# Two trunk layers on one core: the cached context's keys and values of the second mixer expanded between the last expert and the first projection

## The reference, cut to what matters

```python
def mla_expand(ckv, kpe, w_ukv, g_k):
    kv = (ckv @ w_ukv).reshape(bn, n, C_HEADS, C_NOPE + C_V)
    k_nope, v = kv[..., :C_NOPE], kv[..., C_NOPE:]
    k = jnp.concatenate([k_nope, jnp.broadcast_to(kpe[:, :, None, :], ...)], -1)
    return rms_norm(k, g_k), v

# odd_mixer
z = h @ p['w_in']                                # 1024 -> 384 + 256 + 32
q = rms_norm((rms_norm(cq, p['g_qa']) @ p['w_uq']).reshape(bn, n, C_HEADS, C_QK), p['g_q'])
k, v = mla_expand(rms_norm(ckv, p['g_kva']), kpe, p['w_ukv'], p['g_k'])
...                                              # rotary positions for latent tokens
kc, vc = mla_expand(ctx[0], ctx[1], p['w_ukv'], p['g_k'])
out = dense_attention(q, concat([kc, k]), concat([vc, v]), C_SCALE, None)
```

## Time and profile before

| what | value |
|---|---|
| median of 3 runs | 1086.15 us (1083.31 to 1087.44) |
| the profiled execution | 1081.3 us |
| its span in the profile | 1079.5 us |
| PE busy | 913.2 us, 85% |
| DVE busy | 387.9 us, 36% |
| ACT busy | 238.7 us, 22% |
| POOL busy | 120.6 us, 11% |
| bytes moved | 324.97 MB, mean 301 GB/s |
| granted TensorE clock, mean | 0.926 of full |

### The profile page before, as it was taken

The page is one execution under the profiler, slowest core; times in us unless marked ns, Lnnn a source line. Parts: engine busy times, 40 slices in busy tenths (PEclk is TensorE's granted clock), DMA queues, the critical chain, the costliest instruction groups (busy, mean ns, idle before and its releaser), DMA issues.

```text
span 1079.5 us, 14089 instructions
## 1 busy us (share of the span) xinstructions
PE 913.2 (85%) x5389; PEld 522.4 (48%) x5389; DVE 387.9 (36%) x1096; ACT 238.7 (22%) x598; POOL 120.6 (11%) x131
## 2 busy tenths in 40 slices
PE   5999798977999985998399979997869998859980
PEld 2346346446555553554165544553565555525540
DVE  1112565246522120221334665661456222212214
ACT  3110143120111110111334454341111111101111
POOL 1000001000222211121000000001001222112210
PEclk9999899987999997998699997998869999989996
DMA  9979897385989998998740057008499899999984
GB/s 379 399 294 403 318 417 308 103 276 211 373 313 401 415 416 361 416 413 343 297 149 6 1 193 275 10 7 286 181 404 366 330 410 417 416 392 409 413 338 182
DMA packets 69835, 324.97 MB, mean 301 GB/s; under 512 B 12566, under 2 KB 13590, under 8 KB 46600
## 3 DMA queue, kind: packets, MB, share of 16 engines
q1 hardware_dynamic: 54016, 291.99, 68.0%
q0 software_dynamic: 13328, 25.02, 6.8%
q10 hardware_dynamic: 2432, 7.17, 1.7%
HBM read 318.97 MB, written 26.49 MB: 320 GB/s over the span
## 4 chain that ended last, share of the span: by engine, by line
PE 64%; DMA 21%; DVE 9%; ACT 2%; issue 2%; SPq 1%; POOL 0%; POOLq 0%; DVEq 0%; ACTq 0%
PE psum L760 16%; DMA ring<-in_l_w 13%; PE psum L773 8%; PE psum L956 7%; PE psum L710 4%; DMA ring<-in_l_w_ada 3%; PE psum L1048 3%; PE psum L740 2%; PE psum L1057 2%; PE psum L1008 2%; PE psum L601 2%; PE psum L1089 2%; PE psum L723 1%; DMA scale_shift<-gate_rows_hbm 1%; PE psum L731 1%
## 5 line engine op out<-in xcount | busy, mean ns | idle before, releaser
L760 PE MATMUL psum<-ring,scratch 128*64 128x256 f32 x1920 | 226.8, 390 | 24.6 <-DMA ring<-in_l_w 22.8
L760 PEld LDWEIGHTS psum<-ring,scratch 128*64 128x64 f32 x1920 | 143.6, 140 | 92.9 <-issue 35.2
L1902 DVE TENSOR_TENSOR scratch<-scratch,psum 64x256 f32<-64x256 f32 x64 | 27.2, 424 | 315.0 <-ACT scratch L1304 314.9
L773 PE MATMUL psum<-ring,scratch 128*64 128x512 f32 x496 | 119.9, 604 | 2.6 <-ACT scratch L1308 1.9
L2336 POOL DMA_INDIRECT expert_rows<-scratch,slot_rows x64 | 63.7, 995 | 333.2 <-ACT scratch L1318 321.5
L1304 ACT ACTIVATE scratch<-psum 64x256 f32<-64x256 f32 x64 | 24.0, 375 | 258.4 <-PE psum L760 258.4
L956 PE MATMUL psum<-ring,scratch 128*128 128x512 f32 x192 | 73.1, 539 | 1.3 <-DVE scratch L2023 1.3
L1318 ACT COPY scratch<-psum 128x512 f32<-128x512 f32 x64 | 37.5, 586 | 146.8 <-PE psum L773 146.8
L601 PE MATMUL psum<-ring,scT 128*32 128x512 f32 x320 | 42.9, 662 | 14.7 <-DMA ring<-in_l_w_ada 13.6
L956 PEld LDWEIGHTS psum<-ring,scratch 128*128 128x128 f32 x192 | 36.1, 190 | 36.5 <-issue 35.5
L773 PEld LDWEIGHTS psum<-ring,scratch 128*64 128x64 f32 x496 | 31.0, 136 | 44.9 <-issue 39.9
(11 more groups left out here) (316 smaller groups left out, 1152.0 us busy)
## 6 DMA issues: line engine op xcount, KB each, us to landing
ring<-in_l_w SPq DMA_DIRECT2D x186, 1024.0 KB, 16.6
ring<-in_l_w_ada SPq DMA_DIRECT2D x48, 1024.0 KB, 13.6
ring<-in_l_w_o SPq DMA_DIRECT2D x8, 1024.0 KB, 13.0
ring<-in_l_w_in SPq DMA_DIRECT2D x4, 1024.0 KB, 25.6
gate_rows<-gate_rows_hbm POOLq DMA_DIRECT2D x8, 512.0 KB, 9.8
scale_shift<-gate_rows_hbm POOLq DMA_DIRECT2D x8, 512.0 KB, 11.0
scratch<-expert_rows SPq DMA_DIRECT2D x8, 512.0 KB, 5.0
ring<-in_l_w_in SPq DMA_DIRECT2D x4, 768.0 KB, 13.0
```

The lines of the kernel that those rows point to most:

```text
L760: last = nc.tensor.matmul(ps[64 * n:64 * n + 64, 2 + par, 0:DE], mine[:, k, :], part(w, k * DE, DE), start=k == 0, stop=k == KD - 1)
L773: last = nc.tensor.matmul(ps[64 * n:64 * n + 64, 5 + par, :], hhT[:, par, k, :], part(w2, k * D + n * 512, 512), start=k == 0, stop=k == 1)
```

## The change

Tile 3 comes first in `UNITS` and in `C_ORDER`. Its latents are transposed and both its units expanded on PE right behind the last expert, before `transpose_h` of tile 0; ACT and DVE do `unit(0)` before their part of the first combine and `unit(1)` before `evac_h` of tile 1. Only the `transpose_heads` of these two stay in the loop. SP loads `w_ukv` first of all, then the cached context (until now on ACT's queue), and the state behind that. In the loop `transpose_c(2)` follows `expand(2)`. At the end the third attention item's scores go ahead of the last `transpose_heads`, ACT and DVE do the first item's exponentials and maxima before they empty the last heads, and the query scales are taken in two parts. The first pieces of the last modulation are let go by `e_in_psum` at the last kv unit. PSUM banks, scratch places and counts in waits are moved to match. The diff, cut to its core:

```diff
-        UNITS = [("kv", 0), ("q", 0), ("kv", 3), ("kv", 1), ("q", 1), ("kv", 2), ("q", 2)]
+        UNITS = [("kv", 3), ("kv", 0), ("q", 0), ("kv", 1), ("q", 1), ("kv", 2), ("q", 2)]
...
-        C_ORDER = (0, 1, 3, 2)
+        LAST_KV = max(n for n, u in enumerate(UNITS) if u[0] == "kv")
+        C_ORDER = (3, 0, 1, 2)
...
-            return 4 + n if n < 2 else 2 * (n % 2)
+            return n if n < 2 else 2 * ((n + 1) % 2)
+        def unit_bank(n):
+            return 4 + 2 * n if n < 2 else 2 * ((n + 1) % 3)
...
 # SP
             load_experts(0)
+            for k in range(2):
+                load(U_UKV + k, SLOT, A["l1_w_ukv"][k * P:(k + 1) * P, :])
+            sp.wait_ge(S["up_done"], NE)
+            sp.dma_start(ckvw[:, 3, 0:KV_LORA], ...).then_inc(S["cache_in"], 16)
+            sp.dma_start(ckvw[:, 3, KV_LORA:], ...).then_inc(S["cache_in"], 16)
             load_state(0)
             load_pairs(0)
...
-            for k in range(2):
-                load(U_UKV + k, SLOT, A["l1_w_ukv"][k * P:(k + 1) * P, :])
-            sp.wait_ge(S["units_used"], used(U_UKV + 1))
+            sp.wait_ge(S["e_in_psum"], LAST_KV + 1)
...
 # PE, project1
+                    if k == 6 and t == 1:
+                        pe.wait_ge(S["e_act"], 1)
+                        pe.wait_ge(S["e_squares"], 1)
+                        pe.wait_ge(S["e_dve"], 1)
...
 # PE, transpose_c
-                if n:
-                    pe.wait_ge(S["cT_act"], c_count(C_ORDER[n - 1], (3,)))
-                    pe.wait_ge(S["cT_dve"], n)
-                else:
-                    pe.wait_ge(S["y_evac"], NE + 2)
+                if t == 0:
+                    pe.wait_ge(S["e_act"], 2)
+                    pe.wait_ge(S["e_squares"], 2)
+                    pe.wait_ge(S["e_dve"], 2)
+                elif t == 1:
+                    pe.wait_ge(S["cT_act"], 1)
+                    pe.wait_ge(S["cT_dve"], 2)
+                elif t == 2:
+                    pe.wait_ge(S["c_read"], NT)
...
 # PE, expand
-                if n < 3:
-                    pe.wait_ge(S["c_read"], n + 1)
-                    pe.wait_ge(S["c_raw_dve"], n + 1)
+                if n < 2:
+                    pe.wait_ge(S["y_evac"], NE + 1 + n)
+                elif n < 5:
+                    pe.wait_ge(S["c_read"], n - 1)
+                    pe.wait_ge(S["c_raw_dve"], n - 1)
...
+            transpose_c(3)
+            expand(0)
+            expand(1)
             transpose_h(2, h3, 0)
             project1(0)
             project1(1)
             transpose_c(0)
             project1(2)
             transpose_c(1)
-            transpose_c(3)
-            expand(0)
-            transpose_c(2)
-            expand(1)
             for n in range(len(UNITS)):
                 if n + 2 < len(UNITS):
                     expand(n + 2)
+                if n == 0:
+                    transpose_c(2)
                 if n >= len(UNITS) - 2:
                     scores1(n + 2 - len(UNITS))
+                if n == len(UNITS) - 1:
+                    scores1(2)
                 transpose_heads(n)
-            scores1(2)
...
 # ACT
-            act.wait_ge(S["down_done"], NE)
-            act.dma_start(ckvw[:, 3, 0:KV_LORA], ...)
-            act.dma_start(ckvw[:, 3, KV_LORA:], ...)
...
+            act.wait_ge(S["cache_in"], 32)
+            link(nc.scalar.activation(junk[:, 0:ROPE], ckvw[:, 3, KV_LORA:], ACT.Square, ...))
+            unit(0)
             scale_pair(0, 0)
             scale_pair(0, 1)
             rms(2, (0,))
             evac_h(2, hT, 0)
             scale_pair(0, 2)
             rms(2, (1,))
+            unit(1)
             evac_h(2, hT, 1)
...
-            for n in range(len(UNITS)):
+            for n in range(2, len(UNITS)):
                 unit(n)
-                if n:
+                if n == 2:
+                    evac_heads(0)
+                if UNITS[n][0] == "kv":
                     evac_heads(n - 1)
+            exps1(0)
             evac_heads(len(UNITS) - 1)
-            exps1(0)
...
 # DVE
+            evac_c(3)
+            dve.wait_ge(S["cache_in"], 32)
+            link(V.tensor_tensor(kr[:, 3, :], ckvw[:, 3, KV_LORA:], gkr, ALU.mult))
+            unit(0)
+            combine(0, 0)
             norm(2, 0)
             evac_h(2, hT, 0)
             combine(0, 1)
             norm(2, 1)
+            unit(1)
             evac_h(2, hT, 1)
...
-            for n in range(len(UNITS)):
+            for n in range(2, len(UNITS)):
+                if n == len(UNITS) - 2:
+                    query_scales(0, 2)
                 unit(n)
+            maxima1(0)
             evac_heads(len(UNITS) - 1)
-            dve.wait_ge(S["q_roots"], NT)
-            link(V.reciprocal(s1[:, 136:184], s1[:, 136:184]))
-            link(V.tensor_scalar(s1[:, 136:184], s1[:, 136:184], QK ** -0.5, None, ALU.mult))
-            maxima1(0)
+            query_scales(2, 3)
```

More of the change, by code:

```diff
@@ L262, in trunk @@
         late = ring[:, 9:12, :].rearrange("p s n -> p (s n)")
[L263 to L267, removed]
+        cqw = view(late, 32, NT, Q_LORA)
+        ckvw = view(late, 1184, 4, KV_LORA + ROPE)
+        kw = view(late, 2336, 3, HALF, QK)
+        ckvT = view(late, 4640, 4, 2, P)
+        junk = view(late, 5664, Q_LORA)
         cqT = view(ring[:, 0, :], 0, NT, 3, P)
@@ L277, in trunk @@
         sq1 = view(W, 8192, 2, HALF * QK)
+        sq_cache = view(AB, D, 2, HALF * NOPE)
         probs1 = view(W, 8192, 2, 768)
@@ L1018, in transpose_c @@
                 n = C_ORDER.index(t)
+                q_bank, kv_bank = (4, 5) if t == 2 else (6, 7)
                 if t < 3:
@@ L1459, in evac_c @@
                 act.wait_ge(S["cT_in_psum"], C_ORDER.index(t) + 1)
+                bank = 4 if t == 2 else 6
                 for k in range(3):
-                    last = nc.scalar.activation(cqT[:, t, k, :], ps[:, 6, k * P:(k + 1) * P], ACT.Identity,
+                    last = nc.scalar.activation(cqT[:, t, k, :], ps[:, bank, k * P:(k + 1) * P], ACT.Identity,
                                                 scale=cols[:, G1_AT + k:G1_AT + k + 1])
@@ L1483, in unit @@
                         .then_inc(S["e_squares"], 1)
+                    evac_heads(n - 1)
                     if hb == 1:
@@ L2104, in _ @@
             dve.wait_ge(S["gains_ready"], 1)
-            combine(0, 0)
             def read_c(t):
@@ L2123, in evac_c @@
                     return
+                bank = 5 if t == 2 else 7
                 for k in range(2):
-                    last = V.tensor_scalar(ckvT[:, t, k, :], ps[:, 7, k * P:(k + 1) * P],
+                    last = V.tensor_scalar(ckvT[:, t, k, :], ps[:, bank, k * P:(k + 1) * P],
                                            cols[:, G1_AT + 3 + k:G1_AT + 4 + k], None, ALU.mult)
@@ L2141, in unit @@
                 kind, t, hb = UNITS[n]
-                parts = head_parts(kind, n % 3)
+                parts = head_parts(kind, unit_bank(n))
                 mine = kw[:, n % 3, :, :]
-                sums = sq1[:, n % 2, 0:HALF * (NOPE if kind == "kv" else QK)].rearrange("p (h c) -> p h c", h=HALF)
+                sums = squares_of(n)[:, 0:HALF * (NOPE if kind == "kv" else QK)].rearrange("p (h c) -> p h c", h=HALF)
                 if kind == "kv":
@@ L2150, in unit @@
                         .then_inc(S["e_sums"], 1)
-                    if n:
+                    if n == 2:
+                        evac_heads(0)
+                    if n > 1:
                         evac_heads(n - 1)
@@ L2271, in _, with query_scales @@
                                    op0=ALU.mult, op1=ALU.mult).then_inc(S["kv_out"], 1)
-            for n in range(len(UNITS)):
+            def query_scales(first, last):
+                dve.wait_ge(S["q_roots"], last)
+                part = s1[:, 136 + 16 * first:136 + 16 * last]
+                link(V.reciprocal(part, part))
+                link(V.tensor_scalar(part, part, QK ** -0.5, None, ALU.mult))
+            for n in range(2, len(UNITS)):
+                if n == len(UNITS) - 2:
+                    query_scales(0, 2)
                 unit(n)
+            maxima1(0)
             evac_heads(len(UNITS) - 1)
-            dve.wait_ge(S["q_roots"], NT)
-            link(V.reciprocal(s1[:, 136:184], s1[:, 136:184]))
-            link(V.tensor_scalar(s1[:, 136:184], s1[:, 136:184], QK ** -0.5, None, ALU.mult))
-            maxima1(0)
+            query_scales(2, 3)
             for n in range(len(ATT1)):
```

43 lines of the change are left out of this document (22 added, 21 removed).

## The result

The changed kernel takes 1075.25 us in the median of 4 runs (1070.98 to 1075.74), the kernel before 1085.97 (4 runs). The ratio is 0.9886, interval 0.9852 to 0.9921. Run again beside the experiments, unaltered, it gave 1075.02 against 1085.88, ratio 0.9904 (0.9871 to 0.9936). Forecast were 1076.8 us, and a gain of 9.3.

What follows compares the result with a forecast made beforehand. PE carried 64% of the chain and transfers 21%, so time comes off where PE is waited for. Terms -8.3, -1.5, 0 and +0.5 sum to -9.3 us: 1086.15 to 1076.8 us, range 1070.3 to 1082.8.

Steps and rivals of the forecast that it cites:

- Term 1: PE-bound stretch behind the projections: two expansions (6.9 us) move into the gap, 1.4 us of waits around them go; -8.3 us.
- The wait that I had put at 0 to 0.5 us: Possible new PE wait: transpose_heads(1) needs evac_heads(0), which ACT and DVE reach only inside unit(2); taken as 0.
- Term 2: Last expansion to last head transposes: PE's wait on ACT goes, 7.4 us becomes 5.9; -1.5 us.
- Term 3: Behind the heads: w_o moves with them, and its 15.9 us to modulation piece 2 hide ACT's added work; 0 us.
- my own sign: Forecast wrong if, among other signs, piece 2 came less than 15.9 us behind w_o or did not move with the heads.
- Term 4: Gap between last down-projection and first tile's transposes: state transfer shares with the last result rows; +0.5 us, bounds 0 and 3.4.
- cold expansions: In the gap: at half clock the first expansion takes 6.9 us and unit(0) ends 1.9 us late, delaying the combine.
- A: Clock stays full through the gap as PE idles about 8.4 us; 2.3 us more gained, 1074.5 us; chance 0.12.
- B: Gap: cached rows land late, clock falls, unit(0) holds up the combine; 1079.7 us, or 1081.5 with more sharing; chance 0.16.
- C: Projections behind the gap stay at half clock; gain gone if it returns about 560, 1092 us if at 572; chance 0.03.
- D: Behind the heads: gain hidden or given back, as w_o waits for something else or a tail wait appears; about 1084; chance 0.06.

Runs made afterwards that it cites:

- the tail alone: Kernel before, with only third item's scores and ACT's evac_heads moved earlier, first exponentials and maxima before the last heads are emptied, query scales split: 1082.86 against 1084.74 us (0.9975).
- the early release alone: Changed kernel with the end-of-loop reordering undone (third scores, ACT's evac_heads, exponentials, maxima, query scales): 1078.42 us against 1084.74 for the kernel before (0.9952).
- The order alone: Kernel before with only SP's load order changed: w_ukv behind the last expert's loads, state held until the last up-projection is through; 1086.59 against 1085.88 us (1.0001).

## Why the prediction was right, and where it was not

**Term 1 (-8.3).** 62.91 to 54.55 us behind the projections: 8.36, in every version that has the moved expansions (54.54 or 54.55). The wait that I had put at 0 to 0.5 us isn't there.

**Term 2 (-1.5).** 7.40 to 5.63: 1.77, shown by the tail alone as well. The wait on ACT was the cause as said; the pieces up to the last heads are each a little shorter than the 1.0 us that I gave them (two scores 1.95 together), 0.3 in all.

**Term 3 (0).** The shift came through `w_o` as argued: what follows the heads kept its length within 0.8 us, with PE waiting 3.70 on ACT before piece 0 under that cover, and took 4.6 us less as soon as `w_o` was out of the way. The 0.8 us (15.95 to 15.19 and 15.12) I had not foreseen, and by my own sign, piece 2 at less than 15.9 behind the heads, they speak against the term, though they are a fifth of what `w_o` was worth. The tail alone has most of them (15.26) with the old release of pieces 0 and 1, and the early release alone has most of them too (15.32, without the tail), so neither is needed; the cause stays open.

**Term 4 (+0.5, bounds 0 and 3.4).** This is the step that was mis-sized: the gap grew by 2.24 and 2.43 us. The argument (state in flight across the last result rows) was right and its size was not. I had bounded sharing by 1.5 us; it cost the rows 1.8 to 2.2 and the row pairs another 0 to 0.5. The order alone, with nothing else changed, costs 2.0, and putting the state first takes 1.9 off the time to the row pairs' issue.

I had the state in by 519, 3.1 us after the last down-projection; its last load landed at 523.6 or later, 4.3 us after it or more. One reason is on the record: I gave `w_ukv` a lead of 14.0 us over the last down-projection (501.9 to 515.90), and it had 11.8, mostly because the up-projection at half clock that the profile before has in between (5.36 us) took 3.67 in both profiles after. The first combine, for which I had given 10 us after the last down-projection within 1, came at 12.09, and PE's idle time ahead of the transposes was 9.49 instead of 8.

The sentence from the Trainium skill, "DMA: Bandwidth & Descriptors", section "Queues, rings and completion order", that rings take turns on each engine, pointed to near 1.5 rather than 0.5, and the runs side with it. They also agree with what it says of order within a ring: in the changed kernel the slower load of `w_ukv` landed by 519.6 and the cached rows behind it at 520.1. That a ring of their own brings them sooner they don't show: with the state first they land 2.2 us after the last down-projection on either. The other part of the term, cold expansions, did not occur in the two profiles of the change (7.10 us for 16 matmuls), but did in one of the two others that have its order of loads (8.80).

**The sum.** Gap +2.24, projections -0.87, heads -8.36 and -1.77, behind them -0.76: -9.5 us against -9.3. Two errors of opposite sign, 1.8 more in the gap and 1.0 less behind the last q expansion, hide each other; the 0.87 is where the clock came back, and in the second profile it is +0.59. There the same sum is +2.43 +0.59 -8.37 -1.77 -0.83 = -7.95, and another 2.08 are gained behind piece 2, in the stretch that scatters. So the mechanisms of terms 1 and 2 are shown, and that the total lies within a few tenths of the forecast is in part luck.

**The rivals.** A (clock survives) did not happen; its price of 2.3 us stands as plausible, as full clock took 1.5 to 3.0 us off the stretch in the one profile that had it. B in full, with the combine held back, happened not in the change but in four neighbours of it; its cold expansions without the delay in a fifth. The first cold expansion took 5.4 us there and not 6.9, as the clock came back during it. C did not: the clock was full from about 544. D neither.

## What to carry to other kernels

Work with no dependence on what PE waits for was worth its full length here when it moved out of a PE-bound stretch into an idle one, and the profile before gave that figure to the tenth. The cost is in what has to come along: the weights and small inputs that must now be there earlier, and the transfers that they push over the next short transfer on the path. Price those by moving only the order of loads; here the order alone cost 2.0 us, beside the 10 that the change gained in all. And an input that lands 1 us before it would cost something has no margin: look at more than one profile before calling it hidden.

## What was not expected of the hardware

The cached rows, two loads of 144 KB together, pay for the traffic around them and not for their size. Counted from the second issue they landed in 1.9 us at rest, 4.9 to 5.3 behind 2 MB of weights on SP's queue, 6.31 behind the same weights when these came later, 8.54 behind the state as well, and 4.19 and 6.76 on ACT's queue beside the weights on SP's; issued later on ACT's, they were there no sooner. And the clock was lost after short waits, not always after the same ones: it was full through the expansions that began 1.92 and 2.14 us after the last down-projection and half in those that began after 2.30, and an idle time of 3.24 us ahead of the transposes, after 14 us of dense matmuls, was enough to lose it as they began.
